# A streaming encoder layer on one core: the down projection of the second token group as seven block products

## What is computed

```
h = x + W_o [SWA_sink_GQA(n) ; DiffAttn(n)],  n = RMSNorm(x)
y = RMSNorm(h + SwiGLU(RMSNorm(h)))

def swiglu(h, w_gate, w_up, w_down):
    g = jnp.einsum('bsd,df->bsf', h, w_gate)
    u = jnp.einsum('bsd,df->bsf', h, w_up)
    return jnp.einsum('bsf,fd->bsd', jax.nn.silu(g) * u, w_down)
```

## Time and profile before

| | |
|---|---|
| median of 3 runs | 2715.58 us (2713.7 to 2716.72) |
| profiled execution: time, span | 2712.58 us, 2710.7 us |
| granted clock of TensorE, mean | 0.981 |
| PE busy | 2551.7 us, 94% |
| DVE, ACT, POOL busy | 1838.8, 1210.9, 608.9 us (68, 45, 22%) |
| L2858 to L2860, gate and up | 1848 matmuls each |
| L2873 to L2875, down, both groups | 748 matmuls each |
| L2341, the adds of down | 374, 748 ns each |

### The profile page before, as it was taken

How to read it: one execution, slowest core, us unless ns; L and a number is a source line. 1 busy time by engine, 2 the same in 40 slices (tenths; PEclk the granted TensorE clock), 3 DMA queues, 4 the chain that set the end, 5 groups by cost and what they waited for, 6 DMA issues and landing times.

```text
span 2710.7 us, 48183 instructions
## 1 busy us (share of the span) xinstructions
PE 2551.7 (94%) x19292; PEld 1584.9 (58%) x19292; DVE 1838.8 (68%) x3586; ACT 1210.9 (45%) x2117; POOL 608.9 (22%) x610
## 2 busy tenths in 40 slices
PE   3999999978899999898899999999999999999998
PEld 1566666656667766554344444444467777666665
DVE  8777777758888774676887878876764444444445
ACT  4566666657889999443232223322441111111112
POOL 1211111104666667222212111110320000000001
PEclk9999999997999999999999999999999999999999
DMA  4113311133220000533453334433412222222221
GB/s 182 61 64 106 110 57 59 59 88 72 38 37 10 9 6 9 183 125 109 155 173 138 117 117 148 173 139 117 155 40 74 84 85 86 79 71 70 71 82 71
DMA packets 149872, 245.81 MB, mean 91 GB/s; under 512 B 47298, under 2 KB 102002, under 8 KB 148114
## 3 DMA queue, kind: packets, MB, share of 16 engines
q1 hardware_dynamic: 149650, 242.74, 27.0%
HBM read 148.83 MB, written 90.94 MB: 88 GB/s over the span
## 4 chain that ended last, share of the span: by engine, by line
PE 50%; DVE 4%; issue 2%; ACT 2%; DMA 1%; POOL 1%; POOLq 0%; SPq 0%; DVEq 0%; ACTq 0%
PE bank L2858 10%; PE bank L2859 9%; PE bank L2860 9%; PE bank L2873 6%; PE bank L2874 6%; PE bank L2875 6%; PE bank L2810 1%; PE bank L2812 1%; PE bank L2811 1%; PE bank L2791 1%; DMA tail_buffers<-mix_scratch 1%; PE bank L2780 1%; DVE tail_buffers L2283 1%; DVE tail_buffers L2173 0%; DVE residual_rows L2188 0%
## 5 line engine op out<-in xcount | busy, mean ns | idle before, releaser
L2858 PE MATMUL bank<-ffn_inT_sums,tail_buffers 128*128 128x512 f16 (+2 forms) x1848 | 578.3, 313 | 4.4 <-DVE tail_buffers L2283 3.0
L2859 PE MATMUL bank<-ffn_inT_sums,tail_buffers 128*128 128x512 f16 (+2 forms) x1848 | 578.3, 313 | 0.0
L2860 PE MATMUL bank<-ffn_inT_sums,tail_buffers 128*128 128x512 f16 (+2 forms) x1848 | 578.2, 313 | 0.0
L2341 DVE SCALAR_TENSOR_TENSOR residual_rows<-bank,pair_scales,residual_rows 128x512 f32<-128x512 f32 (+1 forms) x374 | 273.2, 748 | 116.0 <-PE bank L2875 115.5
L2873 PE MATMUL bank<-tail_buffers 128*128 128x512 f16 (+1 forms) x748 | 285.4, 382 | 12.9 <-DVE residual_rows L2341 7.4
L1095 PE MATMUL z_ps<-w_in_hi_lo,normT_hi 128*128 128x384 f16 x816 | 268.3, 329 | 21.9 <-DVE w_in_hi_lo L682 21.9
L2874 PE MATMUL bank<-tail_buffers 128*128 128x512 f16 (+1 forms) x748 | 285.0, 381 | 0.0
L2875 PE MATMUL bank<-tail_buffers 128*128 128x512 f16 (+1 forms) x748 | 285.0, 381 | 0.0
L1096 PE MATMUL z_ps<-w_in_hi_lo,normT_hi 128*128 128x384 f16 x816 | 268.2, 329 | 0.0
L1097 PE MATMUL z_ps<-w_in_hi_lo,normT_lo 128*128 128x384 f16 x816 | 268.0, 328 | 0.0
L2858 PEld LDWEIGHTS bank<-ffn_inT_sums,tail_buffers 128*128 128x128 f16 x1848 | 181.0, 98 | 104.8 <-issue 5.2
(11 more groups left out here) (333 smaller groups left out, 5156.0 us busy)
## 6 DMA issues: line engine op xcount, KB each, us to landing
gate_up_scratch<-tail_buffers SPq DMA_DIRECT2D x77, 512.0 KB, 3.2
tail_buffers<-gate_up_scratch SPq DMA_DIRECT2D x77, 512.0 KB, 3.5
tail_buffers<-in_w_gate SPq DMA_DIRECT2D x22, 512.0 KB, 5.3
tail_buffers<-in_w_up SPq DMA_DIRECT2D x22, 512.0 KB, 6.3
tail_buffers<-in_w_down SPq DMA_DIRECT2D x22, 512.0 KB, 5.9
down_scratch<-tail_buffers SPq DMA_DIRECT2D x22, 512.0 KB, 3.2
tail_buffers<-down_scratch SPq DMA_DIRECT2D x22, 512.0 KB, 4.4
keys_values<-in_w_in SPq DMA_DIRECT2D x8, 1152.0 KB, 15.9
```

What stands on the lines that cost most here:

```text
L2341: nc.vector.scalar_tensor_tensor(out, BK[y_bank(e, y)][0:rows, :], PS[0:rows, i, F_YI:F_YI + 1], out, ALU.mult, ALU.add).then_inc(h_ok, 1)
L2858: nc.tensor.matmul(out, wh, nh, start=first and k == 0, stop=False, skip_group_check=True)
L2859: nc.tensor.matmul(out, wh, nl, start=False, stop=False, skip_group_check=True)
L2860: last = nc.tensor.matmul(out, wl, nh, start=False, stop=k == 3, skip_group_check=True)
```

## The change

Down of group 2 gets seven block products too, for pairs 0 to 9 (`D_PAIRS`). Hidden halves and token halves are the blocks of the left operand, hidden halves and output halves those of the weight. That needs sums on both sides:

- **Group 1** makes four sums of each down weight pair: POOL `down_sums` (four operations 128x512, in place in `DW`, from the moment `down_lo` is done), ACT `down_sum_hi`, DVE `down_sum_lo`, SP `store_sum`. Since the sums overwrite `DW`, `load_down(i + 1)` now waits for the last `down_sum_lo` of pair i. There are three staging buffers for four sums; the fourth waits for the store of the first. Pairs 0 and 1 have orders of their own.
- **Group 2** makes four sums of the activations per block (DVE `act_sum`, ACT `act_sum_hi`, DVE `act_sum_lo`), 256 columns each.
- The residual of the prompt half tiles is kept in another basis: X4 takes all six products that enter every block, X2 and X3 take the differences. `change_basis` (DVE, 128x512 on SBUF alone) goes into it in pair 0 (8 operations) and out of it in the last down phase (8).
- Down of pair i becomes 30 **slots** (`SLOTS`): 28 of three matmuls and two for the stream tokens of six. One slot stands behind each gate/up product of pair i+1, a 15th at the end of each block, in banks 6 and 7 alone; slot s waits for the add of slot s-2. The last pair's down stays as it was, as 18 half tiles at the end.

```diff
+                def down_sums(i):
+                    pool.wait_ge(d_lo, 2 * i + 2)
+                    (b11, b12), (b21, b22) = ([DW[f][:, half[n]] for n in range(2)] for f in range(2))
+                    nc.gpsimd.tensor_tensor(b11, b12, b11, ALU.subtract).then_inc(tw_ok, 1)
+                    pool.wait_ge(tw_ok, 4 * i + 1)
...
@@ block.gpsimd, the order over the pairs of group 1
-                    if i > 1 and more:
+                    if i and more:
                         max_gate_up(i + 1)
                     max_down(i)
+                    if i == 0:
+                        max_gate_up(1)
                     if i < 2:
-                        max_gate_up(i + 1)
                         weight_sums(i + 1)
+                    if i < D_PAIRS:
+                        down_sums(i)
                     if i and i + 2 < PAIRS:
                         weight_sums(i + 2)
...
+                def act_sum(n, k):
...
+                    nc.vector.tensor_tensor(sums[k], left, right, how).then_inc(s_ok, 1)
+                def act_sum_lo(i, b, n, k):
+                    dve.wait_ge(sh_ok, 4 * (n - PAIRS) + k + 1)
...
+                def down_sum_lo(i, k):
+                    dve.wait_ge(th_ok, 4 * i + k + 1)
...
+                    nc.vector.scalar_tensor_tensor(lo, v, ps(i, F_D), hi, ALU.mult, ALU.subtract).then_inc(tl_ok, 1)
+                def change_basis(tp, x):
+                    v, w = basis_region(tp, x), basis_region(tp, X4)
+                    nc.vector.tensor_tensor(v, w, v, ALU.subtract).then_inc(cv_ok, 1)
...
+                def add_slot(i, n):
+                    dve.wait_ge(y_ok, y_base(1, i) + n + 1)
...
@@ block.vector, group 1
                     if i == 1:
+                        for k in range(4):
+                            down_sum_lo(0, k)
                         slot_lo(1, 5)
                         slot_lo(1, 6)
...
                     block_22(0, i, 512, 0)
...
                     if i == 1:
-                        slot_lo(2, 0)
+                        gate_up_scales(2)
+                        down_scales(1)
                     sum_3(0, i, 512, 1)
                     block_22(0, i, 512, 1)
...
                     if steady:
                         slot_lo(i + 1, 3)
+                        down_sum_lo(i, 0)
...
+                def down_sum_hi(i, k):
+                    act.wait_ge(tw_ok, 4 * i + k + 1)
+                    if k == 3:
+                        act.wait_ge(tw_st[0], 16 * (i + 1))
...
@@ block.scalar, end of pair 0
                     for j in range((0, 3, 6)[min(i, 2)], 7) if more else ():
+                        if i == 0 and j == 5:
+                            for k in range(4):
+                                down_sum_hi(0, k)
                         slot_hi(i + 1, j)
...
+                def down_slot(i, s_):
...
+                    if i or s_ > 1:
+                        pe.wait_ge(h_ok, y_base(1, i) + s_ - 1)
+                    out = BK[6 + s_ % 2]
...
+                    nc.tensor.matmul(out[:, :], ah, wh, start=first, stop=False, skip_group_check=True)
+                    nc.tensor.matmul(out[:, :], ah, wl, start=False, stop=False, skip_group_check=True)
+                    nc.tensor.matmul(out[:, :], al, wh, start=False, stop=True, skip_group_check=True).then_inc(y_ok, 1)
...
@@ block.tensor, group 2
+                                if i:
+                                    down_slot(i - 1, 15 * b + 2 * j + x)
+                        if i:
+                            down_slot(i - 1, 15 * b + 14)
```

More of the change, by code:

```diff
@@ L2038, in _ @@
                             load_gate_up(i + 2, j // 5)
+                        if i > 1 and j == 4:
+                            for k in range(3):
+                                store_sum(i, k)
+                        if i > 1 and j == 5:
+                            store_sum(i, 3)
+                            load_down(i + 1)
+                    if i == 1:
+                        for k in range(4):
+                            store_sum(1, k)
+                        load_down(2)
                     if i + 2 == PAIRS:
@@ L2452, in _ @@
                     block_21(0, i, 512, 0)
-                    act_lo(0, 0, i, 512, 1)
+                    if steady:
+                        down_sum_lo(i, 1)
+                    act_lo(0, i, 0, i, 512, 1)
                     if i == 0:
@@ L2518, in _ @@
                         block_12(1, n, w, 0)
-                        act_lo(1, b, n, w, 2)
+                        adds(12)
+                        act_lo(1, i, b, n, w, 2)
                         if tail:
@@ L2861, in gate_up, with sample_down @@
                     last.then_inc(gu_ok, 1)
+                def sample_down(i, n, out):
+                    for f in range(2):
+                        ah, al = (A1S(i, h)[:, f, :] for h in range(2))
+                        nc.tensor.matmul(out, ah, DH1[:, f, half[n]], start=f == 0, stop=False)
+                        nc.tensor.matmul(out, ah, DL1[:, f, half[n]], start=False, stop=False)
+                        last = nc.tensor.matmul(out, al, DH1[:, f, half[n]], start=False, stop=f == 1)
+                    last.then_inc(y_ok, 1)
                 def down(e, i, y):
                     t = tiles(e)[y // 2]
-                    rows = P if t < NT else DEC
                     if y >= 4:
@@ L2869, in down @@
                         pe.wait_ge(h_ok, y_base(e, i))
-                    out = BK[y_bank(e, y)][0:rows, :]
+                    out = BK[y_bank(e, y)]
+                    if t == TS:
+                        sample_down(i, y % 2, out[0:DEC, :])
+                        return
                     for f in range(2):
-                        ah, al = (A[e][:, f, a_cols(t)] for A in (AH, AL))
-                        nc.tensor.matmul(out, ah, DH[:, f, half[y % 2]], start=f == 0, stop=False)
-                        nc.tensor.matmul(out, ah, DL[:, f, half[y % 2]], start=False, stop=False)
-                        last = nc.tensor.matmul(out, al, DH[:, f, half[y % 2]], start=False, stop=f == 1)
```

407 lines of the change are left out of this document (320 added, 87 removed).

## The result

| | before | after |
|---|---|---|
| median of the runs | 2714.64 us (2708.8 to 2716.72, 4 runs) | 2737.98 us (2735.31 to 2738.59, 4 runs) |
| profiled execution | 2712.58 us, span 2710.7 | 2735.31 us, span 2733.5 |
| mean granted clock | 0.981 | 0.977 |

The ratio is 1.0088, with a 95% interval of 1.007 to 1.0105: 0.9% slower. The forecast was 2734 us, the range 2701 to 2750.

What follows compares the result with a forecast made beforehand. PE was taken to bound both groups, busy throughout. Terms -25.9 + 2.3 + 3.7 + 21 + 5 + 14.5 = +20.6 on 2712.6 gave 2733.2, plus 1 for the median: 2734 us; own range 2712 to 2750, with rivals 2701 to 2750.

Steps and rivals of the forecast that it cites:

- group 2: matmuls, ways in and out, slots: Group 2's down: 120 matmuls fewer, -25.9 us; extra ways in and out of the 64-token steps, +2.3; slots, 0.
- last down phase: Last pair's down: six `change_basis` of about 0.6 us on a full DVE, +3.7 us, bounds 2 and 6.
- steady pairs of group 1: Pairs 3 to 9: later `act_lo` holds up down, y4 waits too; 3.0 us a pair, +21, bounds 7 and 28.
- pair 2: Group 1: late `load_down(2)` delays the first `sum_2` some 2 us, plus a steady pair's 3.0; +5, bounds 2 and 8.
- pairs 0 and 1: Group 1's start: y4, `copy_1` and small operations beside POOL's sums come late; +14.5 us, bounds 6 and 20.
- third rival: Group 2: with two banks late adds stop PE, 0.1 us in each of 300 slots; 2763 us, chance 0.10.
- fourth rival: Group 2: first matmul behind each change of kind costs extra, 560 of 0.02 us, 11; 2745 us, chance 0.05.
- the queue of three `down_sum_lo`: Steady pairs: three `down_sum_lo` stand in DVE's queue ahead of `act_lo` number 2, 2.1 us.
- the turns with POOL: Steady pairs: DVE operations wait for POOL's second sum (+0.9 us) and fourth (+1.15), as SBUF operations exclude each other.
- the 5 us kept for the first block and the rest: Allowances beside zero cost: up to 3 us for group 2's first block, at most 2 for copies, stores and loads.
- first rival: Group 1 has the room: new work falls into DVE's waits, only the first pairs pay; 2699 us, chance 0.20.
- The second: Rival for group 1: places are right, but DVE and POOL do not exclude each other; 2710 us, chance 0.15.

Runs made afterwards that it cites:

- e6: As e4, but the eight `change_basis` of the last down phase left out, output not the reference's: 2692.0 us, ratio to before 0.9917.
- e2: Changed kernel without POOL's four `down_sums` of a pair, rows copied as they are, output not the reference's: 2719.0 us, ratio to before 1.0020.
- e3: Changed kernel without DVE's four `down_sum_lo` of a pair, high part stored twice, output not the reference's: 2717.5 us, ratio to before 1.0016.
- e4: Changed kernel with group 1's old order, POOL's sums after the last `slot_lo`, DVE's low parts at the next pair's start, same result: 2692.7 us.
- e7: Changed kernel with `gate_up_scales(2)` moved ahead of the first `sum_3` in pair 1, same result: 2739.7 us, ratio to before 1.0089.
- e8: Changed kernel without POOL's four weight sums for pair 2, which lie in pair 1, output not the reference's: 2732.7 us, ratio to before 1.0069.
- e1: Kernel before with only group 2 changed, loading stored down weights instead of sums, output not the reference's: 2694.9 us, ratio to before 0.9929.

## Why the prediction was right, step by step

| step | forecast | measured | by |
|---|---|---|---|
| group 2: matmuls, ways in and out, slots | -23.6 | -23.7 | pair of 60.09 us |
| last down phase | +3.7 | +3.7 | from its first matmul to the last norm row; e6 |
| wait ahead of it, and first products of group 2 | nothing | +1.1, +0.2 | PE's timeline |
| steady pairs of group 1 | +21 (3.0 each) | +24.3 (3.5 each) | PE's timeline |
| pair 2 | +5 | +5.5 | PE's timeline |
| pairs 0 and 1 | +14.5 | +13.4 | PE's timeline |
| between the groups: a higher clock in the one profile | nothing | -1.7 | PE's timeline, granted clock |
| sum | +20.6 | +22.8 | spans |

Group 2, the steady pairs and the last down phase cost what they do in the way that was forecast; pairs 0 to 2 came to their sum by other ways. That the sum is off by only 2 us is in part luck: the clock was put at nothing, and chains that were forecast too long made up for it.

*Group 2* came as worked out from the pitch. The pair of 59.9 us in the prediction's last paragraph leaves out its own 0.23 for the ways in and out; with it, it is 60.1, and 60.09 was measured. That 300 slots with two banks cost nothing (the third rival) stood on DVE's 44 of 60 us; the stage has 397 of 562, 42 a pair. It holds up to the last slot; behind that, PE waits 0.95. The fourth rival is out too.

*Steady pairs.* Both terms, the queue of three `down_sum_lo` and the turns with POOL (0.9 and 1.15 forecast; 0.93 and 1.05 measured against 1.27), are shown by e2, e3 and e4. PE waited 2.04 ahead of down, where I had 2.55, so my chain was 0.5 too long; the wait at y4 is 0.42 or 0.78, forecast 0.5. What I had at nothing is the clock. The three pairs at full clock lose 2.8, 3.2 and 2.8 us, as forecast. In the other four, down runs for 22.4 us and not 21.3 to 21.7, and they lose 3.9 each. Three of the seven downs, windows of the changed kernel, two at 0.92 and one at 1.00:

```profile
1797.50:1820.00 22.50, 22.45 (x97) 9.91 (x98) 18.55 (x22) 3.27 (x5) 9.38 (x4) 0.92 0.50 177
1496.20:1517.50 21.30, 20.88 (x97) 9.31 (x98) 18.36 (x22) 3.17 (x5) 9.40 (x4) 1.00 0.52 185
1858.40:1880.80 22.40, 22.38 (x96) 9.82 (x97) 15.99 (x21) 3.24 (x5) 0.00 (x0) 0.92 0.66 247
```

*Pair 2* has the right sum by another way. The first `sum_2` was not 2 us late: it began 19.4 us after the pair's first product, before the change 20.1, and no product waited. All of the wait, 3.76 us, stands ahead of down, where POOL's sums held one `slot_lo` (2.33) and one `down_sum_lo` (1.75). The other 2.8 us are the down behind it, 23.5 us long instead of 20.7, at a granted clock of 0.88.

*Pairs 0 and 1* have the right sum with a wrong middle. Pair 0 lost 0.3 us, forecast 1.7: y4 waited 1.27 longer, but fewer matmuls were slow behind it. p3's wait is `copy_1` behind the fourth `down_sum_hi`, as said: 1.73, forecast 2.3. This is ACT's timeline (L2839 `down_sum_hi`, L2847 `copy_1`), which answers the earlier trace rows:

```profile
1324.62 0.72 ACT L2839 ACTIVATE tail_buffers<-tail_buffers,pair_scales 128x512 f16<-128x512 f32 x1 [15.30 <-DMA down_sums_scratch<-tail_buffers]
...
1327.33 1.06 ACT L2847 ACTIVATE tail_buffers<-bank 128x512 f32<-128x512 f32 x2
```

p12 was to be 8 to 9 us late, because four or five small operations would wait 2 us each beside POOL. It was 4.79 late. POOL's sums began at 1350.71, not 1349.5, so they met only the end of the chain, and of that two operations:

```profile
1352.07 0.99 DVE L2392 TENSOR_TENSOR pair_fields<-pair_fields 128x1 f32<-128x1 f32 x1
...
1353.47 1.90 DVE L2394 CAST pair_fields_int<-pair_fields 128x2 int32<-128x2 f32 x1
```

The `TENSOR_SCALAR` operations between them kept their 0.15. The rest came later, ahead of down: `slot_lo` and two `down_lo` took 6.6 us beside POOL. Down began at 1371.36, forecast 1374, and ran 1.7 us longer, at a granted clock of 0.92.

What was forecast did happen in e3, where POOL's sums began with the cast L2383, 0.02 us behind its start, and not 0.43 behind it. Four of the small operations waited, and p12 came 9.21 us late. The first two:

```profile
1350.30 2.38 DVE L2383 CAST pair_fields_int<-pair_fields 128x4 int32<-128x4 f32 x1
1352.71 2.27 DVE L2384 TENSOR_SCALAR pair_scales<-pair_fields_int 128x4 int32<-128x4 int32 x1
```

Yet that pair's products took 50.1 us there, and 50.5 after: `slot_lo` and `down_lo` then stood behind POOL's sums and not beside them. So the explanation had the wrong lever. I named the place of the scales as the cause; e7 moved them and won nothing, e8 shows that DVE's turns with POOL's weight sums are half of it.

*The range.* The bounds of the terms add up to 2707 and 2752 us, and to 2757 with the 5 us kept for the first block and the rest; 2712 to 2750 is narrower, without a reason given. The result lies inside either.

*The first rival* (group 1 has the room, 2699 us) was wrong for this order. But e4 shows that the room was there: 89 us of idle in 400, of which it uses part of the 6.2 us at the start of a pair. I had written that this idle lies at the start and not ahead of `act_lo`. It was right of this kernel, and it was also the way to a better one. *The second* (no turns, 2710) is refuted by the `slot_lo` of 2.20 and by e2.

## What to carry to other kernels

Ask of preparation work not only if its engine has room in the stage, but what stands behind it in its queue and how much slack that has. Here some 4 us of new work and turns, ahead of a consumer with 1.5 us of slack and idle, cost 3.5 us in each pair; the same work in the idle time a third of a pair later cost nothing. Two costs share one slack: each alone nearly fits into it, and together they are paid. Removing either then brings back more than its half (17 and 15 of 24 us here), so only the run without either (e1), and the one with both at another place (e4), tell how they add. Where VectorE operations with two SBUF inputs lie beside GpSimd sums on SBUF, count their times as one queue; in e7, moving a chain ahead in it only moved the wait.
